# A top-k mask added to the bias by GpSimd instead of TensorE, index scores in reversed rows, and attention outputs turned in the value banks, in a streaming-encoder step

## The reference, cut to what matters

```python
dots = einsum('bthe,bse->bths', q_idx, kidx) * IDX_DIM ** -0.5
score = einsum('bth,bths->bts', w_idx * N_IDX_HEADS ** -0.5, relu(dots))
score = where(admissible, score, NEG_INF)
_, idx = top_k(score, 256)                       # keys of each query
logits = einsum('bthd,btkd->bthk', q_a, k_a[idx]) * HEAD_DIM ** -0.5 + bias
y_a = einsum('bthk,btkd->bthd', softmax(where(valid, logits, NEG_INF)), v_a[idx])
```

## Time and profile before

| | |
|---|---|
| median of 3 runs | 1910.09 us (1903.37 to 1910.16) |
| the profiled execution | 1911.76 us, of which 1909.8 us are the core's span |
| stretches of the profiled execution | gate tiles until 531.3, branch A 531.5 to 762, branch B 765 to 911, then mix, output and feed-forward |
| TensorE busy | 1814.1 us (95%) |
| VectorE, ScalarE, GpSimd busy | 947.0, 638.8, 470.0 us |

### The profile page before, as it was taken

How to read it: one execution, slowest core, us unless ns; L and a number is a source line. 1 busy time by engine, 2 the same in 40 slices (tenths; PEclk the granted TensorE clock), 3 DMA queues, 4 the chain that set the end, 5 groups by cost and what they waited for, 6 DMA issues and landing times.

```text
span 1909.8 us, 30260 instructions
## 1 busy us (share of the span) xinstructions
PE 1814.1 (95%) x11176; PEld 1722.1 (90%) x11176; DVE 947.0 (50%) x2302; ACT 638.8 (33%) x1237; POOL 470.0 (25%) x269
## 2 busy tenths in 40 slices
PE   7599999999979998899999999999999999999996
PEld 2498999999968897777999999999999999999995
DVE  1547888889135555556565443232323232323234
ACT  3345566641243444444331241212121212121222
POOL 0331222224210011111333222222222222222220
PEclk9699999999998989899999999999999999999998
DMA  7420124242441221754444111111111111111112
GB/s 270 139 61 23 57 91 113 91 128 80 126 109 46 69 69 40 187 149 122 138 135 149 44 34 45 45 45 44 44 44 44 44 44 44 39 44 39 44 44 94
DMA packets 179321, 153.47 MB, mean 80 GB/s; under 512 B 20240, under 2 KB 162016, under 8 KB 178688
## 3 DMA queue, kind: packets, MB, share of 16 engines
q1 hardware_dynamic: 175328, 137.31, 25.1%
q10 hardware_dynamic: 3920, 15.19, 2.0%
HBM read 127.34 MB, written 25.19 MB: 80 GB/s over the span
## 4 chain that ended last, share of the span: by engine, by line
PE 84%; DVE 6%; ACT 4%; DMA 3%; issue 2%; POOL 1%; SPq 0%; DVEq 0%; ACTq 0%; POOLq 0%
PE psum L788 65%; PE psum L1063 5%; PE psum L1054 3%; PE psum L912 2%; PE psum L1081 2%; PE psum L945 2%; PE psum L1026 1%; PE psum L826 1%; PE psum L1027 1%; DVE h_f L1557 1%; DMA ada_c<-in_w_ada 1%; PE psum L1030 1%; DVE u_lo L1927 1%; DMA out<-y_out 1%; DVE score L1614 1%
## 5 line engine op out<-in xcount | busy, mean ns | idle before, releaser
L788 PE MATMUL psum<-h_hi,w_hi 128*128 128x362 f32 (+2 forms) x1440 | 474.6, 330 | 2.5 <-DVE h_lo L1905 1.6
L788 PE MATMUL psum<-h_lo,w_hi 128*128 128x362 f32 (+2 forms) x1440 | 474.1, 329 | 0.0
L788 PE MATMUL psum<-h_hi,w_lo 128*128 128x362 f32 (+2 forms) x1440 | 473.5, 329 | 0.0
L729 POOL CAST w_hi<-w_raw 128x1024 fp32r<-128x1024 f32 x112 | 124.7, 1114 | 1033.7 <-PEq L792 879.4
L731 POOL TENSOR_TENSOR w_lo<-w_raw,w_hi 128x1024 fp32r<-128x1024 f32 x112 | 281.7, 2515 | 9.0
L788 PEld LDWEIGHTS psum<-h_hi,w_hi 128*128 128x128 f32 x1440 | 271.2, 188 | 3.3 <-DVE h_lo L1905 1.9
L788 PEld LDWEIGHTS psum<-h_lo,w_hi 128*128 128x128 f32 x1440 | 271.4, 188 | 0.0
L788 PEld LDWEIGHTS psum<-h_hi,w_lo 128*128 128x128 f32 x1440 | 271.4, 188 | 0.0
L1889 DVE SCALAR_TENSOR_TENSOR xT<-psum,modT,xT 128x364 f32<-128x364 f32 (+3 forms) x288 | 136.1, 497 | 265.3 <-PE psum L788 265.3
L788 PE MATMUL psum<-u_hi,w_hi 128*128 128x362 f32 (+1 forms) x768 | 253.4, 330 | 3.2 <-DVE u_lo L1927 3.2
L788 PE MATMUL psum<-u_lo,w_hi 128*128 128x362 f32 (+1 forms) x768 | 252.0, 328 | 0.0
(11 more groups left out here) (284 smaller groups left out, 2855.0 us busy)
## 6 DMA issues: line engine op xcount, KB each, us to landing
w_raw<-in_w_in SPq DMA_DIRECT2D x32, 512.0 KB, 4.2
ada_c<-in_w_ada SPq DMA_DIRECT2D x32, 512.0 KB, 4.2
w_raw<-in_w_up SPq DMA_DIRECT2D x32, 512.0 KB, 4.1
w_raw<-in_w_down SPq DMA_DIRECT2D x32, 512.0 KB, 3.4
zT_scratch<-z_out ACTq DMA_DIRECT2D x27, 544.0 KB, 2.7
q_raw<-zT_scratch SPq DMA_DIRECT2D x32, 272.0 KB, 5.2
gate<-zT_scratch SPq DMA_DIRECT2D x16, 544.0 KB, 4.6
ada_w<-in_w_ada SPq DMA_DIRECT2D x4, 2048.0 KB, 9.2
```

The costliest lines, as they stand in the source:

```text
L729: pl.tensor_copy(w_hi[slot][:, :], w_raw[slot][:, :]).then_inc(sem("w_hi_made"), 1)
L788: ins = pe.matmul(bank(b, n), w[:, k, wc], x[:, a, c0:c0 + n], start=(m == 0 and p == 0), stop=(m == len(wk) - 1 and p == 2))
```

## The change

1. **Mask.** `selmask` stays float32 and is made for reversed rows. GpSimd multiplies all of it by a large number once, in place, and then adds it to the bias of every unit that needs it, into one of three buffers `bias_m` (`mask_bias`): two of them lie where `z_out` lay. VectorE adds `bias_m` in place of the bias. The third product L1030 goes, and L1032 too: GpSimd writes the barred half block into `biasA` (`bar_future`). The multiplication waits for `mask_ready` and stands in GpSimd's program between the splits of gate tiles 13 and 14: `splits(8, 2)` becomes `splits(7, 2)`, the multiplication, `splits(1, 2)`. TensorE no longer waits for `mask_ready`.
2. **Reversed rows.** ScalarE and VectorE read the index queries backwards from PSUM; the weights `w_tok` go once through a product with `swap` into `w_rev`.
3. **Outputs of pairs 0 to 2** are turned in parts of three tiles (the last: two and the samples) into the free columns of the value bank that the next unit will use, before the values of the loop's unit are weighed. They have no number in the row of groups any more. ScalarE reads them at the end of its loop (after `q_hi`), VectorE between the bias step and `normalised`, and TensorE waits for that read before the next unit's values.
4. **Queries.** `load_q(2)` is issued before the wait for the cached keys and before `biasB`.
5. GpSimd's query splits are interleaved with the masks: heads 2 to 9 after the masks of the 8th and the 11th unit of a pair.

```diff
@@ GpSimd: the weight splits and the new mask work
-            splits(8, 2)
+            splits(7, 2)
             pl.wait_ge(sem("w_split"), 2 + jobs.n)
-
-            for hh in range(16):
+            pl.wait_ge(sem("mask_ready"), 1)
+            pl.tensor_scalar(selmask[:, :], selmask[:, :], -NEG_R, None, ALU.mult).then_inc(sem("mask_scaled"), 1)
+            splits(1, 2)
+            pl.wait_ge(sem("w_split"), 2 + jobs.n)
+            pl.wait_ge(sem("mask_scaled"), 1)
+
+            def split_q(hh):
+
                 q = q_hl[q_slot(hh)]
                 pl.wait_ge(sem("q_hi"), hh + 1)
...
+            def bar_future(pair, half):
+
+                pl.wait_ge(sem(f"biasA_in{half}"), 16 * (pair + 1))
+                pl.memset(biasA[half][64:P, SEQ - CHUNK:SEQ], NEG).then_inc(sem(f"biasA_ready{half}"), 1)
+                pl.wait_ge(sem(f"biasA_ready{half}"), pair + 1)
+
+            def mask_bias(u):
+
+                for piece, c0, w in u["pieces"]:
+                    k = masked[piece]
+                    if k >= 3:
+                        pl.wait_ge(sem("piece_biased"), masked_pieces[k - 3] + 1)
+                    if u["blk"] is None:
+                        pl.wait_ge(sem("biasS_in"), 32 * (u["pair"] + 1))
+                        m0 = SEL_SAMPLE + c0
+                        ins = pl.tensor_tensor(bias_m[k % 3][:, 0:w], biasS[:, c0:c0 + w], selmask[:, m0:m0 + w], ALU.add)
+                    else:
+                        m0 = SEL_OFF[u["blk"]]
+                        for lane, h in enumerate(u["heads"]):
+                            c = lane_at(u, lane)
+                            ins = pl.tensor_tensor(bias_m[k % 3][:, c:c + w], biasA[h % 2][:, SEQ - w:SEQ],
+                                                   selmask[:, m0:m0 + w], ALU.add)
+                    ins.then_inc(sem("bias_masked"), 1)
+                    made.next()
+
+            made = Count()
+            split_q(0)
+            split_q(1)
+            for slot in range(2):
+                pl.wait_ge(sem(f"z_stored{slot}"), 16 * 15)
+            pl.wait_ge(sem("tok_done"), 4)
+            pl.wait_ge(sem("kA_lo_done"), 1)
+            split_after = {starts[hh // 2 - 1] + 7 + 3 * (hh % 2): hh for hh in range(2, 10)}
+            for u in units[:NA]:
+                m = u["n"] - starts[u["pair"]]
+                if m in (0, 4):
+                    if u["n"]:
+                        pl.wait_ge(sem("bias_masked"), made.n)
+                    bar_future(u["pair"], m // 4)
+                if u["blk"] is None or u["blk"] >= 2:
+                    mask_bias(u)
+                if u["n"] in split_after:
+                    pl.wait_ge(sem("bias_masked"), made.n)
+                    split_q(split_after[u["n"]])
+            for hh in range(10, 16):
+                split_q(hh)
@@ TensorE: logits
-            for name, v in (("tok_done", 4), ("kA_lo_done", 1), ("mask_ready", 1), ("cacheV_in", 16), ("cacheA_in", 32)):
+            for name, v in (("tok_done", 4), ("kA_lo_done", 1), ("cacheV_in", 16), ("cacheA_in", 32)):
...
-                            masked = u["br"] == "a" and (u["blk"] is None or u["blk"] >= 2)
-                            diag = u["br"] == "a" and not masked and cc + n == w
                             pe.matmul(out, q, khi, start=True, stop=False)
-                            ins = pe.matmul(out, q, klo, start=False, stop=not (masked or diag))
-                            if masked:
-                                m0 = (SEL_SAMPLE if u["blk"] is None else SEL_OFF[u["blk"]]) + c0 + cc
-                                ins = pe.matmul(out, swap_r[:, :], selmask[:, m0:m0 + n], start=False, stop=True)
-                            if diag:
-                                ins = pe.matmul(psum_w[:, out0 + w - P:out0 + w], swap_r[:, :], diag_r[:, :],
-                                                start=False, stop=True)
+                            ins = pe.matmul(out, q, klo, start=False, stop=True)
@@ TensorE: outputs of branch A, heads pairs 0 to 2
+            def turn_outputs_a(n, pair, part):
+
+                pe.wait_ge(sem("y_done"), n)
+                for m, t in enumerate(units[starts[pair + 1] - 1]["turn"][part][1]):
+                    w = P if t < NBLK else DEC
+                    ins = pe.transpose(bank(6 + (n + 1) % 2)[:, (m + 1) * P:(m + 1) * P + w], y_tok[pair_slot(pair)][0:w, t, :],
+                                       ident[0:w, 0:w])
+                ins.then_inc(sem("y_turned"), 1)
...
                 if u["n"] >= 2:
                     pe.wait_ge(sem("y_done"), u["n"] - 1)
+                for pair, part in turned_after(u["n"] - 1):
+                    if pair < 3:
+                        pe.wait_ge(sem("y_turn_read"), 3 * pair + part + 1)
...
+                for pair, part in turned_after(n):
+                    if pair < 3:
+                        turn_outputs_a(n, pair, part)
                 if n > NA:
                     weigh_all(units[n - 1])
@@ ScalarE and VectorE: reading the turned outputs
+            def turn_hi_a(n, pair, part):
...
+                ac.wait_ge(sem("y_turned"), 3 * pair + part + 1)
+                for at_ps, c0, w in y_spans(n, part):
+                    ins = ac.activation(blocks(y_hi[0][:, pair, c0:c0 + w], w), forward(psum_w[:, at_ps:at_ps + w], w), ACT.Copy)
+                ins.then_inc(sem("y_turn_hi"), 1)
...
+                for pair, part in turned_after(n):
+                    if pair < 3:
+                        turn_lo_a(n, pair, part)
                 if n != NA:
                     normalised(u if n < NA else units[n - 1])
@@ VectorE: the bias step of branch A
-                        dv.wait_ge(sem(f"biasA_in{h % 2}"), 16 * (u["pair"] + 1))
+                        dv.wait_ge(sem(f"biasA_ready{h % 2}"), u["pair"] + 1)
...
+                        if piece in masked:
+                            k = masked[piece]
+                            dv.wait_ge(sem("bias_masked"), k + 1)
+                            bias_here = bias_m[k % 3][:, lane_at(u, lane):lane_at(u, lane) + w]
+                        else:
+                            bias_here = bias[:, c0:c0 + w]
                         ins = dv.tensor_tensor_reduce(out=buffer(u)[:, o:o + w], in0=psum_w[:, at_ps:at_ps + w],
-                                                      in1=bias[:, c0:c0 + w], scale=1.0, scalar=-3e38, op0=ALU.add,
+                                                      in1=bias_here, scale=1.0, scalar=-3e38, op0=ALU.add,
@@ SyncE: the third head's queries
+            load_q(2)
             sp.wait_ge(sem("cacheA_turned"), 4)
...
             for pair in range(1, 5):
-                load_q(2 * pair)
+                if pair > 1:
+                    load_q(2 * pair)
                 load_q(2 * pair + 1)
@@ index scores in reversed rows
+            pe.matmul(bank(7, 8 * NBLK + 4), swap[:, :], w_tok[:, :, :].rearrange("p t c -> p (t c)")[:, 0:8 * NBLK + 4],
+                      start=True, stop=True).then_inc(sem("w_turned"), 1)
...
-                    q0 = P * SEL_BLOCKS[grp] - Q0
+                    q0 = SEQ - P - P * SEL_BLOCKS[grp]
...
-                        ins = ac.activation(qI_hl[pair % 2][r, o:o + e - a], bank(b, 512, r)[:, a:e], ACT.Copy)
+                        ins = ac.activation(qI_hl[pair % 2][r, o:o + e - a], bank(b, 512, r)[:, a:e][:, ::-1], ACT.Copy)
...
+            dv.wait_ge(sem("w_turned"), 1)
+            link(dv.tensor_copy(w_rev[:, :, :].rearrange("p t c -> p (t c)")[:, 0:8 * NBLK + 4], bank(7, 8 * NBLK + 4)))
...
-                wt = w_tok[:, tile, h:h + 1]
+                wt = w_rev[:, tile, h:h + 1]
```

More of the change, by code:

```diff
@@ L135, in attention_units @@
             if last and last["blk"] is None:
+                if last["br"] == "a" and last["pair"] < 3:
+                    last.setdefault("turn", []).append((None, list(range(3 * m, 3 * m + 3))))
+                    continue
                 last.setdefault("turn", []).append((group, list(range(4 * m, min(4 * m + 4, NT)))))
@@ L183, in hybrid_step @@
         swap = keep("swap", [P, P])
-        swap_r = keep("swap_r", [P, P], F32R)
-        diag_r = keep("diag_r", [P, P], F32R)
         z_out_at = small[0]
@@ L194, in hybrid_step @@
         w_tok = keep("w_tok", [P, NT, 8])
+        w_rev = keep("w_rev", [P, NT, 8])
         row_sq = keep("row_sq", [P, NT])
@@ L402, in through @@
             return units[n - 1]["pieces"][-1][0] + 1
+        masked = {}
+        masked_pieces = []
+        for u in units[:NA]:
+            if u["blk"] is None or u["blk"] >= 2:
+                for piece, _, _ in u["pieces"]:
+                    masked[piece] = len(masked_pieces)
+                    masked_pieces.append(piece)
         pieces = []
@@ L1126, in _ @@
                 for pair, part in turned_after(n):
-                    turn_outputs(pair, part)
+                    if pair >= 3:
+                        turn_outputs(pair, part)
                 if n + 1 == NA:
@@ L1516, in _ @@
```

(5 more changed lines are left out.)

44 lines of the change are left out of this document (29 added, 15 removed).

## The result

The changed kernel takes 1927.8 us (median of 4 runs, 1925.0 to 1931.6), the kernel before 1910.1: a ratio of 1.0104 over the recorded runs, with an interval of 1.0079 to 1.0129 (the two medians alone give 1.0093). So it is slower by 1%, and the forecast of 1924 is close. But two of its terms are wrong by about 11 us each, in opposite directions. The profile shows where.

The account below looks back on a forecast made before the run. TensorE, busy in 95% of the span, sets the end unless it waits; branch A's loops also hang on chains between engines. 15.7 + 6.6 − 9.8 − 12.4 + 7 + 7 + 0.3 = +14.4 on 1910.1: 1924 us, range 1916 to 1933.

Parts of the forecast that it names:

- Part 1: Gate tile 14: its weight split waits behind GpSimd's mask multiplication (5.5 us), TensorE waits 13.5, lower clock 2.2; +15.7 us.
- slower rival: GpSimd's mask multiplication at the two-input rate, 13.2 us, or GpSimd as the bound: +22, about 1932 us; chance 0.22.
- Part 2: Start of branch A: first bias step waits for its masked bias, +5.0, and lower clock, +1.6; together +6.6 us.
- Part 3: Pair 0: queries loaded earlier give back 5.7, lower-clock products 2.4, shorter later loops 1.7; together −9.8 us.
- Part 4: Pairs 1 to 3: fewer mask products and turned outputs −3.6, full clock kept −8.8; −12.4 us, then +7 for clock falls.
- two falls of the clock: Branch A: TensorE's longer waits lower the clock twice, at 3.5 us each; +7 us (0 to 12).
- 24.0 us stay 24: Pair 3, loops of units 1 to 7: 1.4 us gained up to unit 4 is lost again in it.
- Part 5: Branch A: GpSimd holds VectorE's paired negated maxima through the shared port, 8 at some 0.9 us; +7 us (0 to 12).
- Part 6: Small terms: the product with `swap` and copy to `w_rev` +0.3 us; backward reads, branch B and mask setup at nothing.
- the index part: The product with `swap` and the copy to `w_rev` delay the first weighing by some 0.4 us; counted as +0.3.
- The first rival: Pauses but no loss in branch A: clock stays high, maxima miss GpSimd; +0.4, about 1910 us; chance 0.27 with the last rival.
- the third: The rival with GpSimd's mask multiplication at 13.2 us, or GpSimd as the bound: +22, about 1932 us; chance 0.22.

Follow-up runs that it names:

- e4: e1 with the mask multiplication cut into four pieces and a two-tile product, a copy and an addition of a number beside it; one execution took 1909.1 us.
- e5: e1 with the first masked bias made before GpSimd splits head 1's queries, in another buffer; 1895.7 us, 0.9936 of the kernel before.
- e3: The kernel before with only the third head's queries loaded sooner; 1902.7 us, 0.9977 of the kernel before.
- e8: The kernel before with e3's edit and branch A's outputs turned in the value banks, the mask still on TensorE; 1899.3 us, 0.9941.
- e7: The kernel before, unchanged, run for a second profile; that execution took 1909.3 us.
- e1: The changed kernel with GpSimd's mask multiplication moved after the split of gate tile 15; 1899.4 us, 0.9955 of the kernel before.
- e6: e1 with each negated maximum of two lanes done as two of one lane; 1897.7 us, 0.9930 of the kernel before.

## Why the prediction came out as it did

**Part 1** (+15.7): the mechanism was right in every step, the price was wrong. The multiplication was put between 5.5 and 13.2 us and lasted 16.2, outside both bounds. The step that failed: the lower bound was taken "as it reads one tensor, like the cast", and the upper bound as if two inputs were the dearest case. e4 shows that the number of inputs is not what counts; arithmetic costs 2.4 to 2.8 us per 1024 columns with one input or two, and only plain copies and casts cost 1.0. The stall was 24.1 for 13.5, and 2.7 us more for the lower clock, for which 2.2 were charged. In all +26.8, 11 us more than forecast. (The recorded sum 509.5 + 5.5 + 3.5 is 518.5 and not 518.6, which changes nothing.) By the prediction's own test ("if the multiplication lasts over 9 us") this was the slower rival's case, and its 1932 missed because of the next points.

**Part 2** (+5.0 and 1.6 of clock): the first turn came exactly 5.0 us later behind the logits. e5 confirms the cause; its cure was worth 1.7 us at the start of pair 1 and not 5.0, since the next mask then sets the pace. The lower clock cost less than the 1.6: the first two loops took 9.0 us (569.3 to 578.3) for 8.1 before (536.8 to 544.9). And they took 9.0 in e3 too, after the wait of 2.4 us that the kernel before also has, so this loss does not need the longer wait.

**Part 3** (−9.8): pair 0 became 6.4 us shorter, for 8.2 with part 2's clock. Two sizes failed. The whole wait of 5.73 was taken as gain, but by e3 1.8 of it stays, behind other work of ScalarE. And 2.4 were taken for products at the lower clock, but in e3 that loop and the next give only 1.0 beyond the wait, as the six turns behind it still take 1.49 us (561.35, and 565.49 before). With the two first loops 0.9 longer, pair 0 gained 4.0 there. The rest of the change gave the other 2.4, for 1.7 charged to the mask products.

**Part 4** (−12.4, and +7 for two falls of the clock): two terms were too careful. First, "24.0 us stay 24" for units 1 to 7 was wrong: from the turn of unit 1 to that of unit 7 the changed kernel needs 22.3 us in pair 3 (724.2 to 746.5), and e8, with the turning alone, 21.9. The walk through the units had found a gain and then given it away again in the loop of unit 4; the trace does not (TensorE waits there for `yA_lo`, but 1.1 us in pair 3 and not some 3). Second, the clock. −8.8 assumed that pairs 1 and 2 keep it, which they did, and e7 and e3 show that this is no property of the change: without the mask or the turning pair 2 or both have the full clock in one execution and not in the next. One fall was near in size (4.6 us: 14.7 for 10.1, for two of 3.5) but came at the end of pair 3. In all seven profiles with the mask on GpSimd the samples' first eight probabilities of pair 3 are turned wholly or mostly at the lower clock (in 1.57 to 1.91 us), in the four with the mask on TensorE at the full one (1.04). A wait of 1.5 us of TensorE for ScalarE stands ahead of it in both e1 and e8, so that wait alone does not make the fall; what does is left open.

**Part 5** (+7): the hold beside GpSimd was forecast at 8 maxima of 0.9 us; it was six of 16, 5.0 us in all, and by e6 about half of it was on the path. Right in kind, too large by 4 or 5 us. GpSimd was busy for 30.6 us of a pair, for 31; the masks are 15 additions in a pair and not 13, over the 10560 columns that were counted rightly.

**Part 6**: the index part gave +0.7 for 0.3. Branch B, taken at nothing, gave −3.6. e8 has this gain too (−3.9) and shows that it belongs to the turning. There the turning alters only the count of groups, now even, and with it which engine copies; that this is the reason is argued and not shown apart.

So branch A with parts 4 and 5 was +1.6 in the forecast and −10.1 in the trace, part 1 was 11 too low, and branch B gave 3.6. The forecast came near because these cancel, and a reader should not take it for a proof of its terms. The first rival had the truth on branch A and the third on the multiplication.

## What to carry to other kernels

Before a statement goes into the program of an engine that feeds another one, ask what stands behind it there and when that is wanted; here the same 16 us cost 24 between two splits of weights and nothing after them. Price an operation only by a row of the same kind, since copies, arithmetic with a number and arithmetic of two tiles have prices of their own; where no such row exists, put the bound above the dearest row and not at it. And take work off a full engine only after asking what holds its chain: 114 products less on TensorE were worth nothing that could be measured as long as the masks came late, while the order in which its banks come free and a paired maximum done as two single ones were worth some us each, the latter by a rough measure.

## What the runs showed of the hardware

- GpSimd multiplied or added with a number at 2.5 ns a column and 0.2 us fixed (2.78 us for 1024 columns, 16.2 for 6336), more than for the product of two tiles (2.44 us for 1024) and 2.7 times a copy (1.04 us).
- A VectorE operation of 128 x 2 elements in SBUF, 0.17 us alone, took up to 1.44 us beside GpSimd, until GpSimd's running instruction ended (741.60 + 1.36 in pair 3). Two operations of 128 x 1 with one input took 0.15 each in the same place. One of 128 x 1 with two inputs in SBUF, 0.16 alone, took 2.15 us beside GpSimd.
- The granted clock fell to 1.2 GHz for parts of pairs in one execution and not in the next of the same kernel, and most of a scatter of 19 us between executions goes with the mean clock (correlation −0.88 over 49).
